# Expert weights in slices of 128 input channels, six banks of running sums, and a pass without loops

## What is computed

```
logits = t @ router                       # t: 256 x 1024, router: 1024 x 8
top_v, top_i = lax.top_k(logits, 2)
gate = sum(one_hot(top_i, 8) * softmax(top_v)[..., None], axis=1)
y = 0
for e in range(8):                        # wg, wu: 1024 x 3584, wd: 3584 x 1024
    y = y + gate[:, e:e+1] * ((silu(t @ wg[e]) * (t @ wu[e])) @ wd[e])
```

## Time and profile before

| | us |
|---|---|
| median of 3 runs (lowest, highest) | 2712.51 (2712.36, 2713.87) |
| the profiled execution | 2710.45 |
| its span, from the first instruction to the last | 2708.2 |
| PE busy | 2653.8 |
| DVE busy | 1201.3 |
| ACT busy | 357.5 |

### The profile page before, as it was taken

How to read it: one execution, slowest core, us unless ns; L and a number is a source line. 1 busy time by engine, 2 the same in 40 slices (tenths; PEclk the granted TensorE clock), 3 DMA queues, 4 the chain that set the end, 5 groups by cost and what they waited for, 6 DMA issues and landing times.

```text
span 2708.2 us, 84052 instructions
## 1 busy us (share of the span) xinstructions
PE 2653.8 (98%) x39442; PEld 2173.7 (80%) x39442; DVE 1201.3 (44%) x1924; ACT 357.5 (13%) x746; POOL 18.5 (1%) x28
## 2 busy tenths in 40 slices
PE   8999999999999999999999999989999999999997
PEld 5789666797698476994658966659999999999997
DVE  2678865587788424885357763450000000000011
ACT  2210123100100112000241000520000101000000
POOL 1000000000000000000000000000000000000000
PEclk9999999999999999999999999999999999999999
DMA  7344422554455432544325544349999999999995
GB/s 208 125 153 161 159 106 95 205 163 172 148 187 173 157 124 99 183 149 179 127 90 172 171 174 149 109 163 404 411 410 400 396 412 393 411 396 396 410 399 210
DMA packets 268414, 619.50 MB, mean 229 GB/s; under 512 B 10279, under 2 KB 127277, under 8 KB 255821
## 3 DMA queue, kind: packets, MB, share of 16 engines
q1 hardware_dynamic: 265248, 606.14, 60.6%
q0 software_dynamic: 2400, 10.09, 1.3%
q10 hardware_dynamic: 588, 0.63, 0.1%
HBM read 615.77 MB, written 1.05 MB: 228 GB/s over the span
## 4 chain that ended last, share of the span: by engine, by line
PE 95%; DVE 3%; ACT 2%; DMA 0%; issue 0%; SPq 0%; DVEq 0%; ACTq 0%
PE ps L1222 25%; PE ps L1929 20%; PE ps L1944 10%; PE ps L1274 10%; PE ps L1113 8%; PE ps L1124 7%; PE ps L1310 3%; PE ps L1404 2%; PE ps L1855 2%; PE ps L1911 1%; PE ps L1890 1%; PE ps L1515 1%; PE ps L1639 0%; PE ps L1386 0%; DMA ring<-in_fox_w_in 0%
## 5 line engine op out<-in xcount | busy, mean ns | idle before, releaser
L1929 PE MATMUL ps<-arena,ring 128*64 128x88 f32 x14336 | 550.2, 240 | 2.2 <-issue 2.2
L1929 PEld LDWEIGHTS ps<-arena,ring 128*64 128x64 f32 x14336 | 545.8, 139 | 3.5 <-issue 3.3
L2896 DVE TENSOR_TENSOR arena<-arena,ps 128x352 f32<-128x352 f32 x64 | 30.4, 475 | 706.5 <-PE ps L1929 706.5
L1113 PE MATMUL ps<-xT,ring 128*128 128x256 f32 (+2 forms) x960 | 212.9, 381 | 3.3 <-DVE arena L2319 0.9
L1222 PE MATMUL ps<-arena 128*64 128x128 f32 x3520 | 211.6, 273 | 0.0
L1113 PEld LDWEIGHTS ps<-xT,ring 128*128 128x128 f32 (+2 forms) x960 | 177.3, 186 | 36.3 <-issue 8.5
L1222 PE MATMUL ps<-xT,ring 128*64 128x128 f32 x3520 | 202.6, 273 | 0.0
L1222 PE MATMUL ps<-arena,ring 128*64 128x128 f32 x3520 | 201.9, 273 | 0.0
L1222 PEld LDWEIGHTS ps<-arena 128*64 128x64 f32 x3520 | 196.7, 137 | 0.0
L1222 PEld LDWEIGHTS ps<-xT,ring 128*64 128x64 f32 x3520 | 193.9, 137 | 3.2 <-issue 2.8
L1222 PEld LDWEIGHTS ps<-arena,ring 128*64 128x64 f32 x3520 | 194.4, 137 | 0.0
(11 more groups left out here) (482 smaller groups left out, 2809.0 us busy)
## 6 DMA issues: line engine op xcount, KB each, us to landing
ring<-in_moe_w_gate SPq DMA_DIRECT2D x64, 1792.0 KB, 10.8
ring<-in_moe_w_up SPq DMA_DIRECT2D x64, 1792.0 KB, 11.2
ring<-in_moe_w_down SPq DMA_DIRECT2D x32, 2048.0 KB, 11.3
ring<-in_ffn_w_gate_up SPq DMA_DIRECT2D x44, 1024.0 KB, 5.1
ring<-in_ffn_w_gate_up SPq DMA_DIRECT2D x88, 512.0 KB, 7.0
arena<-in_moe_w_down SPq DMA_DIRECT2D x32, 1024.0 KB, 9.9
ring<-in_ffn_w_down SPq DMA_DIRECT2D x55, 512.0 KB, 6.5
ring<-in_ffn_w_down SPq DMA_DIRECT2D x25, 1024.0 KB, 4.9
```

The costliest lines, as they stand in the source:

```text
L1113: ins = pe.matmul(o, lhsT=w[:, k, c0:c0 + m], rhs=rhs[:, k, :], start=(k == 0), stop=(k == kt - 1))
L1929: ins = pe.matmul(ps[h, bank, c0:c0 + CAP], lhsT=w_f[:, k, h], rhs=xe[:, 4 * kh + k, :], start=(kh == k == c0 == 0), stop=(kh == 1 and k = ...
L2896: dve.tensor_tensor(hid_e[:, c0 * CAP:(c0 + n) * CAP], silu_e[:, c0 * CAP:(c0 + n) * CAP], ps[:, bank, 0:n * CAP], ALU.mult).then_inc(hid_ ...
```

## The change

The pass for the first 88 rows of each expert is written anew for SP, PE, ACT and DVE; the old code stays for the further passes behind the flag.

- An expert's gate and up now come in 16 slices of 128 input channels over all 3584 features (first eight of gate, then eight of up); a partition's run is 14 KB. Down comes in seven pieces of 512 rows, as two runs of 8 KB a partition. The 23 loads of each expert go round six places of 16 KB a partition: four in the ring, two in `arena`.
- PE goes through a slice for all 28 feature blocks before the next slice: the gate sums of all features stand in banks 0 to 5 (five blocks a bank), then the up sums in banks 6, 7, 0, 1, 2, 3. ACT writes SiLU of a gate bank to SBUF (`hid_k`), DVE multiplies it there by the up bank, and the seven down pieces follow, with sums in banks 4 and 5.
- A place is released by the first product of the next slice.
- Scatter of the expert before comes behind the first down piece, gathering of the next expert and turning of places behind the third, and turning of the output behind the first slice of the next expert. One expert is gathered before the pass, not two; `turn_places` uses banks 0 and 1.
- The clearing products are gone: the first products of a bank start its sums.
- All of it is written out for eight experts without loops or conditional blocks on PE, ACT, DVE and SP.

SP:

```diff
+            def k_pass():
+                for e in range(N_EXP):
+                    gate, up, down = (inp[k][0, e] for k in ("moe_w_gate_2", "moe_w_up_2", "moe_w_down_2"))
+                    for j in range(K_PIECES):
+                        slot, uses = k_slot(e, j)
+                        if uses:
+                            sp.wait_ge(k_released[slot], uses)
...
+                        if j < 2 * KD:
+                            w, k = (gate, up)[j // KD], j % KD
+                            dst, src = k_slots[slot][:, 0:K_GU], w[k * P:(k + 1) * P, :]
+                        else:
+                            d = j - 2 * KD
+                            dst = k_slots[slot].rearrange("p (q n) -> p q n", q=2)
+                            src = down[4 * d * P:4 * (d + 1) * P, :].rearrange("(q p s) n -> p q (s n)", q=2, s=2)
+                        sp.dma_start(dst, src).then_inc(k_loaded[slot], 16)
```

PE:

```diff
+                    def slice_products(e, j, banks, full, before_bank):
+                        k = j % KD
+                        w = begin(e, j)[:, 0:K_GU].rearrange("p (q n s) -> p q s n", q=N_F // 2, s=2)
+                        for b, (f0, f1) in zip(banks, HID_BANKS):
+                            if k == 0:
+                                before_bank(b)
+                            for f in range(f0, f1):
+                                c0 = (f - f0) * CAP
+                                for h in HALVES:
+                                    ins = pe.matmul(ps[h, b, c0:c0 + CAP], lhsT=w[:, f // 2, f % 2, h], rhs=xe[:, k, :],
+                                                    start=(k == 0 and f == f0), stop=(k == KD - 1), skip_group_check=True)
+                                    if f == 0 and h.start == 0:
+                                        frees(ins)
+                            if k == KD - 1:
+                                ins.then_inc(full, 1)
...
+                    for e in range(N_EXP):
...
+                        for k in range(KD):
+                            if k in (0, 4):
+                                pe.wait_ge(drained_act, xe_kept[k // 4])
+                            slice_products(e, k, GATE_BANKS, gate_full, claim)
+                            if k == 0 and e > 0:
+                                turn_y(6, False)
...
+                        for k in range(KD):
+                            slice_products(e, KD + k, UP_BANKS, up_full, up_bank)
+                        pe.wait_ge(silu_kept, silu0 + len(HID_BANKS))
+                        for d in range(K_PIECES - 2 * KD):
+                            down_products(e, d)
+                            if d == 0:
+                                pe.wait_ge(hid_ready, hid0 + len(HID_BANKS))
+                                for c in range(2 if e > 0 else 0):
+                                    scatter_k(c)
+                            if d == 2:
+                                pe.wait_ge(dve_to_pe, t.up("dve_to_pe"))
+                                if e < N_EXP - 1:
+                                    xe_kept[:] = [to_act(gather(1 + (e + 1) % 2), 6, 7)[1]] * 2
...
+                                turn_places(0)
```

ACT and DVE:

```diff
+                        for b, (f0, f1) in zip(GATE_BANKS, HID_BANKS):
+                            act.wait_ge(gate_full, t.up("gate_full"))
+                            act.activation(hid_k[:, f0 * CAP:f1 * CAP], ps[:, b, 0:(f1 - f0) * CAP], ACT.Silu)\
+                               .then_inc(silu_kept, 1)
...
+                        for bank, (f0, f1) in zip(UP_BANKS, HID_BANKS):
+                            o = hid_k[:, f0 * CAP:f1 * CAP]
+                            dve.wait_ge(silu_kept, t.up("silu_kept"))
+                            dve.wait_ge(up_full, t.up("up_full"))
+                            dve.tensor_tensor(o, o, ps[:, bank, 0:(f1 - f0) * CAP], ALU.mult).then_inc(hid_ready, 1)
```

More of the change, by code:

```diff
@@ L405, in build, with k_slot @@
         N_PIECES = len(pieces)
+        K_GU, K_DN = F_EXP, 4 * D
+        K_PIECES = 2 * KD + F_EXP // (4 * P)
+        k_slots = [ring_flat[:, i * K_DN:(i + 1) * K_DN] for i in range(4)]
+        k_slots += [arena[:, LATE_AT + i * K_DN:LATE_AT + (i + 1) * K_DN] for i in range(2)]
+        K_OLD = [range(i * K_DN // SLOT, ((i + 1) * K_DN - 1) // SLOT + 1) for i in range(4)]
+        N_F, PER_BANK = F_EXP // P, 512 // CAP
+        HID_BANKS = [(b * PER_BANK, min(N_F, (b + 1) * PER_BANK)) for b in range(-(-N_F // PER_BANK))]
+        GATE_BANKS, UP_BANKS = (0, 1, 2, 3, 4, 5), (6, 7, 0, 1, 2, 3)
+        assert len(HID_BANKS) <= 6
+        hid_k = arena[:, 10752:10752 + N_F * CAP]
+        assert cv.at <= 10752 and 10752 + N_F * CAP <= 15360
+        def k_slot(e, j):
+            n = e * K_PIECES + j
+            return n % 6, n // 6
         PIECE_SLOTS = [range(a // SLOT, (b - 1) // SLOT + 1) for a, b in
@@ L465, in build @@
         ex_loaded = [sem(f"expert_piece_loaded{i}") for i in range(N_PIECES)]
+        k_loaded = [sem(f"expert_slice_loaded{i}") for i in range(6)]
+        k_released = [sem(f"expert_slice_released{i}") for i in range(6)]
+        silu_kept = sem("expert_silu_kept")
         ex_released = [sem(f"expert_piece_released{i}") for i in range(N_PIECES)]
@@ L613, in moe_pass @@
                     done = 0
-                    if b == e == 0:
+                    if b == 1 and e == 0:
                         expert_stretch(gate, up, down, 0, True)
@@ L620, in moe_pass @@
                         t.leave()
-            moe_pass(0)
+            k_pass()
             def store_first(n):
@@ L943, in _, with moe_pass @@
             ln_scale()
-            def moe_pass():
+            def moe_pass(nth):
                 def xe_copy(ks=range(KD)):
@@ L949, in xe_copy, with gate_T_copy, y_turned @@
                     return ins
-                def gate_T_copy():
+                def gate_T_copy(b0=6):
                     full()
                     return act.activation(gate_T[0:CAP].rearrange("p (i n) -> p i n", i=TT),
-                                          ps[0:CAP, 6:8, 4 * CAP:4 * CAP + P], ACT.Copy)
+                                          ps[0:CAP, b0:b0 + 2, 4 * CAP:4 * CAP + P], ACT.Copy)
+                def y_turned(b0):
+                    for c in range(2):
+                        full()
+                        drain(act.activation(y_e[0:CAP, c * 512:(c + 1) * 512], ps[0:CAP, b0 + c, :], ACT.Copy))
                 def y_rows_copy(last=False):
@@ L967, in moe_pass, with yT_copy @@
                     drain(xe_copy(range(4 * b, 4 * b + 4)))
+                def yT_copy(h):
+                    full()
+                    drain(act.activation(yT_e[:, 4 * h:4 * h + 4].rearrange("p a n -> p (a n)"), ps[:, 4 + h, 0:4 * CAP], ACT.Copy))
+                if nth == 0:
+                    for e in range(N_EXP):
+                        if e > 0:
+                            y_turned(6)
+                        for b, (f0, f1) in zip(GATE_BANKS, HID_BANKS):
[3 more added lines that the diff above has]
+                        if e < N_EXP - 1:
+                            full()
+                            drain(xe_copy())
+                        else:
+                            drain(act.activation(small[:, 8:9], eps1, ACT.Copy))
+                        drain(gate_T_copy(0))
+                        for h in range(2):
+                            yT_copy(h)
+                    y_turned(2)
+                    return
                 for e in range(N_EXP):
@@ L1010, in _ @@
             with act.If(more > 0):
-                for _ in range(1, PASSES):
-                    moe_pass()
+                for nth in range(1, PASSES):
+                    moe_pass(nth)
                 last_ln(1)
@@ L1959, in moe_pass @@
                 d_act = t.up("drained_act", 2)
[L1960 to L1964, removed]
                 pe.wait_ge(dve_to_pe, t.up("dve_to_pe"))
@@ L2849, in moe_pass @@
                 find_places(1, 0).then_inc(dve_to_pe, 1)
-                find_places(2, 1).then_inc(dve_to_pe, 1)
                 if b == 0:
+                    find_places(2, 1)
                     gate_weights()
-                find_places(0, 2)
+                else:
+                    find_places(2, 1).then_inc(dve_to_pe, 1)
+                    find_places(0, 2)
                 weigh_places(0)
@@ L2882, in add_last @@
                     then(ins)
+                if b == 0:
+                    for e in range(N_EXP):
+                        for bank, (f0, f1) in zip(UP_BANKS, HID_BANKS):
[3 more added lines that the diff above has]
+                            dve.tensor_tensor(o, o, ps[:, bank, 0:(f1 - f0) * CAP], ALU.mult).then_inc(hid_ready, 1)
+                        if e > 0:
+                            for c in range(2):
+                                for i in range(TT):
+                                    drain(add_one(i, c, 2 * i + c)[1])
+                        dve.wait_ge(places_used, t.up("places_used"))
+                        if e + 2 < N_EXP:
```

(8 more changed lines are left out.)

97 lines of the change are left out of this document (87 added, 10 removed).

## The result

The changed kernel takes 2866.6 us in the median of four runs (2859.4 to 2873.0); the kernel before took 2712.8 beside it (2712.4 to 2713.9). The forecast was 2767 in a range of 2705 to 2835: the sign and the place were right, the size was not. The profiled execution took 2860.7 us, with a span of 2858.8.

The account below looks back on a forecast made before the run. PE's own pace was taken to bound the expert pass, with DMA close behind; 2710.45 + 58 for instruction fetches - 3 of small gains = 2765, plus 2 to the median gave 2767 us, range 2705 to 2835.

Parts of the forecast that it names:

- Products and small gains: Expert pass: products keep 37.92 ns each; dropped clearing products, faster first sweeps and an earlier start save about 3 us.
- Longer runs: Expert-pass weight loads: 14 KB instead of 3.5 KB runs for gate and up are worth 0 while PE is later.
- New waits and handovers: PE after whole gate and up sweeps: SiLU and up products keep up, covered by down's first piece; cost 0.
- rival D: Expert pass: SiLU and products, or next expert's bank claim, end later; 8 to 24 us, 2717 to 2733; chance 0.08.
- Instructions: PE's unlooped expert pass: 166 more packets of 128 products fetched beside full DMA; the wait costs 58 us.
- 166 x 0.35 = 58 us: Expert pass: 166 added instruction packets, each taken to cost PE 0.35 us of waiting.
- 0.62: First loop pass of the kernel before: 3.28 us lost over 5.25 packets, 0.62 us each; 104 us for all.
- 1.11 us: Kernel before, between its two stops: 5.96 us for 128 products needing 4.85; price from above, 184 us in all.
- about 58 us: Sign in the chain: "issue" pieces 128 products apart, about 58 us in all, before gate, up and down products.
- PE's busy time would stay the same within 5 us: Sign on the profile page: PE's busy time unchanged within 5 us while the span grows.
- Rival B: Expert pass: every fetch stops PE; 2893 us at 1.11 us each, 2842 at 0.8; worse at 1.2 GHz; chance 0.13.
- Rival C: Every packet boundary of the expert pass: fetch runs ahead and is hidden, price 0; 2706 to 2709 us; chance 0.24.

Follow-up runs that it names:

- run without weights: The changed kernel, but from the seventh slice on each load brings only 64 numbers a partition, all instructions of PE, ACT and DVE the same: 2707.0 us, ratio 0.9981.
- run cut by columns: The changed kernel with each load cut into four DMAs over all 128 partitions, a quarter of the columns each: 2870.3 us, ratio 1.0582.
- run cut by partitions: The changed kernel with each load cut into four DMAs of 32 partitions, runs as long as before: 3422.4 us, ratio 1.2659.

## Why the prediction was right in its kind and wrong in its size

*Products and small gains:* right in sum; the single gains were not taken apart. The run without weights is 5.6 us faster than before, where the gains (3) and the old stops (2.4) make 5.4. The pass began at 1814.91, expected near 1814.1.

*Longer runs:* worth nothing, as it said; the run cut by columns is the same with 3.5 KB for gate and up.

*New waits and handovers (rival D):* nothing. The waits in front of the pass's products name "issue" alone, and the run without weights has no stop.

*Instructions:* the count (311 packets), the place (128 products apart) and the kind of row ("issue") came as written. **The step that failed is "166 x 0.35 = 58 us".** It measures 0.84 us (the loops of the kernel before written out) to 0.96 us (the changed kernel over its floor), 141 to 160 us. Three things are in it:
- The reason for going down from 0.62, "every stop of PE also stops the release of places, so the DMA queue empties", did not hold. A stop of 1 us is a quarter of the 4.25 us for which one of the six places lasts; the engines stay 84 to 95% busy, 0.88 over the pass, and a load still takes 9.4 us to land, some two transfers deep (1.835 MB at about 350 GB/s take 5.2). The comparison was also made with the wrong row: 10.9 us belongs to the later passes. In the first pass, which gave the 0.62, gate and up landed after 10.0 to 10.3 us, so the changed kernel has about as much in front of a fetch as that pass had.
- 0.62 was itself too low, a mean over a passage of 5.25 packets whose first ones met nearly idle DMA engines, and which was, by the argument of the lead, too short to be past it; the run with the outer loop written out has the same two stops at each expert and then its loop. The row to go by was the 1.11 us of an interval that had a stop, for most packets (7 in 10, as it came out).
- A part of the price was not seen as one: 5.08 us for 128 products in place of 4.85 is 27 us over the 119 stops, in no row of idle time. It stood in the trace of before: of the 1.11 us of an interval, 0.88 was the stop and 0.23 this. The "about 58 us" of issue pieces that were to show it right would not have held it, and its sign that PE's busy time would stay the same within 5 us failed: it grew by 35.6.

*The rivals.* Rival B was nearest: at 0.8 us a packet it stood at 2842. Not every fetch stops PE, though (119 of 166, 7 in 10), and a stop with its restart costs 1.00 + 0.23 = 1.23 us, a little more than the 1.11. Its worst case, a clock at 1.2 GHz, came for some 10 us and cost about 4. The argument against it, two of four packets in time, was drawn from the same short passage. Rival C holds beside idle DMA engines and nearly so at a share of 0.64. It was taken for more likely than B because of the unlooped feed-forward stage, whose half-idle DMA was the objection noted with it; the runs with half and three quarters of the weights show that the objection decides.

*Left open:* why 3 in 10 of the fetches are still in time, mostly in stretches of two or three packets, all through the pass. Seven of the 13 us between the changed kernel and the one with only PE's loops written out. The run cut by columns excludes the length of the runs; the order of the products, the six banks and the other engines' written-out streams were not tried one by one beside full DMA. Of the 37 us of added busy time, the restarts at 0.23 make 27 and the two stretches at the lower clock about 4; six are not accounted for.

## What to carry to other kernels

Before a loop on PE is written out, look at the instruction queue and at the DMA share of the same stretch: packets that are hidden beside half-idle DMA engines become stops beside full ones (here 0.05 us each at a share of 0.64, 0.31 at 0.82, 0.96 at about 0.9). In this pass, bound by PE and by loading at once, the loop was worth keeping; its body of 1,344 instructions was fetched once, and larger bodies were not tried. When a price is taken from the few rows at the beginning of a stretch, ask whether a lead was being used up there, or whether the load beside it had yet begun; here the interval between two stops (1.11 us) was nearer to the steady state than the mean over all packets (0.62).

## What was not expected of the hardware

- Loads of 32 partitions move 221 GB/s with the DMA engines at a share of 1.02; loads of 128 partitions with a quarter of the columns, of the same size, move 346 GB/s at 0.96.
- After a stop for instructions PE needs 5.07 to 5.08 us for its next 128 products in place of 4.85, in every run that has two stops 128 products apart, and as much behind a stop of 0.59 us as behind one of 3.05. In the run cut by partitions some such rows are longer (6.73), in a window whose clock is 0.88.
- Beside full DMA engines an instruction packet of 16.4 KB takes mostly 5.6 to 6.5 us from stop to stop, of which its own transfer is about 1 us, while the same engines bring a load of 448 KB in 5.6 to 6.1 us after its issue (the page of the run cut by columns).
- The granted clock fell to 1.2 GHz for a few us behind two of the longest stops (2.31 and 4.58 us) of the changed kernel; another of 2.24 us at 1987.42 left it at 1.00.
